# Modulation summed into columns on TensorE, and a logarithm's series moved to GpSimd, in a Griffin-style layer

## The chip, the cores and the metric

The kernel runs on one core of a Trainium2 chip, as one program. The metric is the device time of that core in microseconds, the median over several executions. Engines are called by their names in the profile: PE is TensorE (PEld its loads of the stationary operand), DVE is VectorE, ACT is ScalarE, POOL is GpSimd, SP is SyncE, which here only issues DMAs.

## The reference

One layer of a residual trunk on 1024 tokens of width 1024, all in fp32. What the change touches stands at its beginning and in the recurrent branch:

```python
c_act = jax.nn.silu(c)
mod = c_act @ w_ada[l] + b_ada[l]
shift1, scale1, gate1, shift2, scale2, gate2 = jnp.split(mod, N_MOD, axis=-1)
h = _modulated_norm(x, norm_mix_g[l], shift1, scale1)   # rmsnorm(x)*g*(1+scale) + shift
z = h @ w_in[l]
...
log_a = LRU_C * r * jax.nn.log_sigmoid(lam.astype(jnp.float32))
```

`c` is one vector of 1024, so `mod` is a vector times a 1024 x 6144 matrix. `h` feeds a product with 6144 columns, and more products, a scan, a gated mixing and a channel layer follow. `lam` is one number for each of 1024 channels.

## The kernel before, in words

Every engine has its own hand-written instruction stream; semaphores order them. Activations lie transposed, channels in partitions, 1024 tokens in the free dimension, in 8 tiles of 128 channels. Products of weights use three passes with each operand split into a high part (rounded by ScalarE, `hi(n)`, `norm_high(k)`) and a low part (the rest, by VectorE, `lo(n)`, `norm_low(k)`).

The beginning runs like this. SyncE issues `x`, rows of small parameters, then 1 MB halves of `w_ada` with weights between them. TensorE transposes `x` into `x0T`; ScalarE squares it for the norm. VectorE makes `diag0` from the roots of the mean squares, and TensorE broadcasts it (L851) so that ScalarE can keep `rbc0`, the norm's factor of each token, in all partitions.

Of the modulation four parts of 512 columns are needed at the start: part 0 and 2 are halves of the scale, 1 and 3 halves of the shift. Each is a sum over 8 pieces of 128 inputs. `PE_ROWS` gives the pieces of parts 0 and 1 that TensorE takes, as a row: `cact` is the stationary operand and 512 columns of `w_ada` move (`modulation_rows`, L827; an fp32 product is two passes in the trace). VectorE multiplies and adds the other pieces into `part_acc` (`mod_pieces`, L1975 and L1977). `add_row` (L832) adds that accumulator's column sums to the row, ScalarE copies the row to `mod_row` (`row_copy`, L1380), and `row_to_columns` (L837) turns it into four columns of 128 channels with four products. Parts 2 and 3 are all VectorE's, and `part_columns` (L814) sums their accumulators into columns. `mod_columns` (L1986) adds the bias; `scale_columns` also makes `s1`; `normed(k)` (L2007) makes the scaled norm of a tile; `norm_high` (L1384) and `norm_low` (L2012) add the shift and split.

From the first half of scale and shift on, TensorE computes the first gates (`first_gates`, L992 and L985): first those products that need channels of the first half only, then those of the second half. `keep_busy` (L822) is a product whose result nobody reads: one stands ahead of the modulation, and one between the first shift and the first gates.

For the recurrence the logarithm of a sigmoid is worked out on [128, 8] values by a series (`log_start`, `log_terms`, `log_end`, L1950 to L1968), its steps spread over VectorE's stream, each waiting for the one before. POOL makes `ident` and `ones` at the start and then sums of weights (`weight_sums`, L727 to L738), the first of them at 58 us.

Of the kernel before, what the change touches and what calls it, by code (L numbers as in the profile page):

```python
# [11 lines left out]
P = 128  # L12
# [5 lines left out]
def build(nc, a, out):  # L18
# [54 lines left out]
    with ExitStack() as ctx:  # L73
        def sem(name):
            return ctx.enter_context(nc.semaphore(name))
# [53 lines left out]
        mod_row = place("mod_row", [HALF], F32, "T", 2 * TILE + 4 * HALF)  # L129
# [115 lines left out]
        def blocks(t):  # L245
# [10 lines left out]
        rbc_kept, acc_ready, row_sum, row_ready, cols_ready, s1_ready, shift_ready = (  # L256
            sem(x) for x in ("rbc_kept", "acc_ready", "row_sum", "row_ready", "cols_ready", "s1_ready", "shift_ready"))
# [453 lines left out]
        def _(pool):  # L711
# [5 lines left out]

            def weight_sums(item, parts=(0, 1)):
# [51 lines left out]
        def _(pe):  # L770
# [46 lines left out]
            ROW_IN = (ps[3], ps[2])  # L817
            COLS = ps[3][:, 1, :]

            def keep_busy(n, tile):  # L820
                for _ in range(n):
                    nc.tensor.matmul(COLS, ident[:, :], tile, start=True, stop=True)  # L822
# [25 lines left out]
            modulation_rows(0, PE_ROWS[0])  # L848
# [469 lines left out]
        def _(act):  # L1318
# [57 lines left out]
            def row_copy(p):  # L1376
                act.wait_ge(row_sum, p + 1)
                if p:
                    act.wait_ge(cols_ready, p)
                nc.scalar.activation(mod_row[0:1, :], (ps[3], ps[2])[p][0:1, 0, :], ACT.Copy).then_inc(row_ready, 1)  # L1380

# [517 lines left out]
        def _(dve):  # L1899
# [36 lines left out]
            TERMS = 9  # L1936
# [11 lines left out]
            def log_start():  # L1948
                dve.wait_ge(lam_e, 2)
                step(V.tensor_scalar(lt[:, 2, :], lt[:, 1, :], 2.0, None, ALU.add))  # L1950
                step(V.reciprocal(lt[:, 2, :], lt[:, 2, :]))
                step(V.tensor_tensor(lt[:, 1, :], lt[:, 1, :], lt[:, 2, :], ALU.mult))
                step(V.tensor_tensor(lt[:, 2, :], lt[:, 1, :], lt[:, 1, :], ALU.mult))
# [898 lines left out]
```

## Time and profile before

| | us |
|---|---|
| median of 3 runs | 1518.69 (1518.04 to 1519.09) |
| span of the profiled execution | 1517.1 |
| TensorE busy in it | 1498.5 (99%) |
| VectorE busy | 1250.8 (82%) |
| ScalarE busy | 821.4 (54%) |
| POOL busy | 414.0 (27%) |
| first product of the first gates starts | 33.74 |

The profile shows one execution. A row of the timeline gives the start, the time from the first to the last of a run of like instructions, the engine, the line, and in brackets how long the engine had been idle and what ended that. The chain goes back from the last instruction to what released each step. A window's row gives its length, the busy time of PE, PEld, DVE, ACT and POOL with counts of instructions, and the clock that TensorE was granted as a share of 2.4 GHz.

### The profile page before, as it was taken

What the parts mean: (1) busy time and instruction counts of PE and PEld (TensorE: products, weight loads), DVE (VectorE), ACT (ScalarE), POOL (GpSimd) and SP (SyncE); (2) the same over time, 40 slices, a digit from 0 to 9 for tenths busy, and PEclk for the clock granted to TensorE, in tenths of its full rate; (3) what the DMA queues carried; (4) which work ended last, traced back from release to release, by engine and by line L of the source; (5) the groups of instructions that cost most, each with busy time, mean ns of one, the idle gap of its engine ahead of it and who ended that gap; (6) DMA issues with size and microseconds to landing.
All of it is one profiled execution on the core that took longest, in us unless ns stands there. A gap on an engine that the chain in (4) does not pass through costs nothing.

```text
span 1517.1 us, 19716 instructions
## 1 busy us (share of the span) xinstructions
PE 1498.5 (99%) x6770; PEld 1234.8 (81%) x6770; DVE 1250.8 (82%) x1577; ACT 821.4 (54%) x1222; POOL 414.0 (27%) x307
## 2 busy tenths in 40 slices
PE   7999999999999999999999999999999999999998
PEld 4888888888888888888888788888888888888887
DVE  7997888777777786698859999999999987777775
ACT  5378888734454463423446456555555553444447
POOL 0123434523213323000100433333333321333324
PEclk9999999999999999999999999999999999999999
DMA  9532233374443364573421254444444436777722
GB/s 348 186 109 62 67 91 94 116 258 129 160 149 114 102 215 146 174 231 94 167 70 35 63 165 155 153 153 153 153 153 153 153 111 232 250 250 250 250 67 112
DMA packets 212227, 231.12 MB, mean 152 GB/s; under 512 B 9920, under 2 KB 164896, under 8 KB 211360
## 3 DMA queue, kind: packets, MB, share of 16 engines
q1 hardware_dynamic: 212128, 229.86, 45.8%
q8 instruction: 55, 0.90, 0.2%
q14 instruction: 44, 0.36, 0.1%
HBM read 167.95 MB, written 61.87 MB: 151 GB/s over the span
## 4 chain that ended last, share of the span: by engine, by line
PE 92%; DVE 6%; ACT 1%; issue 1%; DMA 0%; DVEq 0%; ACTq 0%
PE ps L886 74%; PE ps L964 4%; PE ps L985 3%; PE ps L1263 1%; PE ps L1110 1%; PE ps L1245 1%; PE ps L1027 1%; PE ps L1167 1%; PE ps L1071 1%; DVE wop L1914 1%; DVE hidw L2616 1%; DVE hq L2559 1%; PE ps L814 1%; DVE n L2551 0%; PE ps L1064 0%
## 5 line engine op out<-in xcount | busy, mean ns | idle before, releaser
L1326 ACT ACTIVATE wop<-raw 128x512 fp32r<-128x512 f32 (+1 forms) x541 | 307.2, 571 | 363.6 <-PE ps L886 240.2
L1914 DVE TENSOR_TENSOR wop<-raw,wop 128x512 fp32r<-128x512 f32 (+1 forms) x541 | 376.4, 699 | 120.1 <-ACT wop L1326 118.5
L727 POOL TENSOR_TENSOR raw<-raw,raw 128x512 f32<-128x512 f32 (+1 forms) x69 | 102.4, 1484 | 868.5 <-DVE wop L1914 423.2
L886 PE MATMUL ps<-hq,wop 128*128 128x512 f32 x888 | 213.9, 390 | 1.1 <-DVE wop L1914 0.9
L886 PEld LDWEIGHTS ps<-hq,wop 128*128 128x128 f32 x888 | 166.3, 188 | 37.6 <-DVE wop L1914 1.3
L886 PE MATMUL ps<-dq,wop 128*128 128x512 f32 x840 | 190.6, 389 | 0.0
L886 PE MATMUL ps<-yq,wop 128*128 128x512 f32 x792 | 190.3, 389 | 0.0
L886 PEld LDWEIGHTS ps<-dq,wop 128*128 128x128 f32 x840 | 157.7, 188 | 32.7
L886 PEld LDWEIGHTS ps<-yq,wop 128*128 128x128 f32 x792 | 148.6, 188 | 30.9
L1928 DVE TENSOR_TENSOR ps<-ps,snap_p 128x512 f32<-128x512 f32 x136 | 94.5, 695 | 48.9 <-PE ps L886 48.3
L1341 ACT ACTIVATE snap_p<-ps 128x512 f32<-128x512 f32 x136 | 81.2, 597 | 98.9 <-PE ps L886 98.8
L2616 DVE SCALAR_TENSOR_TENSOR hidw<-ps,pc,hidw 128x1023 f32<-128x1023 f32 x96 | 122.5, 1276 | 0.9
L734 POOL TENSOR_TENSOR raw<-raw,raw 128x512 f32<-128x512 f32 (+1 forms) x69 | 91.2, 1321 | 93.7 <-DVE wop L1914 92.9
L738 POOL TENSOR_TENSOR raw<-raw,raw 128x512 f32<-128x512 f32 (+1 forms) x69 | 83.5, 1210 | 94.7 <-DVE wop L1914 93.7
L730 POOL TENSOR_TENSOR raw<-raw,raw 128x512 f32<-128x512 f32 (+1 forms) x69 | 94.1, 1363 | 9.9
L964 PE MATMUL ps<-yb_split,wop 128*128 128x512 f32 x288 | 65.7, 389 | 0.0
L1744 ACT ACTIVATE hidw<-ps,pc 128x1024 f32<-128x1024 f32 x48 | 57.5, 1207 | 15.2 <-PE ps L886 12.5
L886 PE MATMUL ps<-t2q,wop 128*128 128x512 f32 x264 | 65.1, 395 | 0.0
L886 PE MATMUL ps<-v4q,wop 128*128 128x512 f32 x264 | 63.6, 390 | 1.0 <-DVE ps L1928 1.0
L886 PE MATMUL ps<-t3q,wop 128*128 128x512 f32 x264 | 64.3, 392 | 0.0
L886 PE MATMUL ps<-t1q,wop 128*128 128x512 f32 x264 | 64.3, 392 | 0.0
L1341 ACT ACTIVATE snap_u<-ps 128x512 f32<-128x512 f32 x62 | 37.0, 598 | 50.2 <-PE ps L886 50.1
(290 smaller groups left out, 2582.2 us busy)
## 6 DMA issues: line engine op xcount, KB each, us to landing
dq<-hid_keep SPq DMA_DIRECT2D x35, 1024.0 KB, 7.3
raw<-in_w_in SPq DMA_DIRECT2D x96, 256.0 KB, 4.1
raw<-in_w_up SPq DMA_DIRECT2D x96, 256.0 KB, 3.3
hid_keep<-part_b SPq DMA_DIRECT2D x40, 512.0 KB, 3.0
hid_keep<-part_t SPq DMA_DIRECT2D x20, 512.0 KB, 3.1
raw<-in_w_down SPq DMA_DIRECT2D x80, 128.0 KB, 2.3
ada_w<-in_w_ada SPq DMA_DIRECT2D x8, 1024.0 KB, 11.4
gate_keep<-tg SPq DMA_DIRECT2D x16, 512.0 KB, 4.5
```

What stands on the lines that cost most here:

```text
L727: nc.gpsimd.tensor_tensor(s1, a21, a22, ALU.add).then_inc(s_made, 1)
L730: nc.gpsimd.tensor_tensor(a21, a11, a21, ALU.subtract).then_inc(s_made, 1)
L734: nc.gpsimd.tensor_tensor(a11, s1, a11, ALU.subtract).then_inc(s_made, 1)
L738: nc.gpsimd.tensor_tensor(s1, a12, a11, ALU.subtract).then_inc(s_made, 1)
L886: done = nc.tensor.matmul(bank, left[:, w, lk, :], right[:, x, rk, :], start=(first and w == 0 and x == 0), stop=(last and w == 1), skip_g ...
L964: done = nc.tensor.matmul(psum[:, h, :], wop[n % 4][:, w, k % KH, :], right(k, x, h), start=(k == 0 and w == 0 and x == 0), stop=(k == KT ...
L1326: nc.scalar.activation(wop[n % 4][:, 0, 0:depth[n], :], raw[slot][:, 0:depth[n], :], ACT.Copy).then_inc(f_hi, 1)
L1341: nc.scalar.activation(dst[:, :], src, ACT.Copy).then_inc(snapped, 1)
L1744: nc.scalar.activation(hidw[slot][:, 1 - s, :], flat(BANKS[pos % 2][s]), ACT.Identity, bias=C("ffn_conv_b", f), scale=C("ffn_conv_w2", f)) ...
L1914: V.tensor_tensor(wop[n % 4][:, 1, 0:kd, :], raw[slot_of[n][0]][:, 0:kd, :], wop[n % 4][:, 0, 0:kd, :].bitcast(F32), ALU.subtract).then_in ...
L1928: V.tensor_tensor(out_b, in_b, kept[:, :], ALU.add).then_inc(joined, 1)
L2616: tap = V.scalar_tensor_tensor(dst[:, d:S], src[:, 0:S - d], C("ffn_conv_w01" if k < 2 else "ffn_conv_w2", k % 2 * 2 * FT + f), dst[:, d:S ...
```

## The change

Parts 0 and 1 are no longer summed as rows. For each piece TensorE loads four 128x128 blocks of `w_ada` as stationary operands and multiplies each with one column of `cact` (`piece_columns`); the results add up in four columns of PSUM, and the accumulator's column sums are added to the same columns (`part_columns`). `mod_row`, ScalarE's two copies of it and the turning into columns are gone. Part 1 has five pieces on TensorE (2 to 6) instead of three (3 to 5), and lies in another PSUM bank than the other parts. Piece 4 of part 0 now stands behind the broadcast. VectorE takes piece 3 of part 0 ahead of the logarithm's beginning, and the order behind it is another; the series from the quotient on runs on POOL ahead of its first weight sum.

```diff
-        PE_ROWS = ((0, 1, 2, 4), (3, 4, 5), (), ())
+        PE_ROWS = ((0, 1, 2, 4), (2, 3, 4, 5, 6), (), ())
...
+        COLUMNS = [(ps[2][:, 0, :] if p == 1 else ps[3][:, 1, :])[:, KH * p:KH * p + KH] for p in range(4)]
...
+            def log_next(ins):
+                logs[0] += 1
+                ins.then_inc(log_step, 1)
+                pool.wait_ge(log_step, logs[0])
+
+            pool.wait_ge(log_root, 1)
+            log_next(nc.gpsimd.tensor_tensor(lt[:, 1, :], lt[:, 1, :], lt[:, 2, :], ALU.mult))
+            log_next(nc.gpsimd.tensor_tensor(lt[:, 2, :], lt[:, 1, :], lt[:, 1, :], ALU.mult))
+            log_next(nc.gpsimd.tensor_scalar(lt[:, 3, :], lt[:, 2, :], 1.0 / (2 * TERMS + 1), 1.0 / (2 * TERMS - 1), ALU.mult, ALU.add))
+            for j in range(TERMS - 2, -1, -1):
+                log_next(nc.gpsimd.tensor_tensor(lt[:, 3, :], lt[:, 3, :], lt[:, 2, :], ALU.mult))
+                log_next(nc.gpsimd.tensor_scalar(lt[:, 3, :], lt[:, 3, :], 1.0 / (2 * j + 1), None, ALU.add))
+            log_next(nc.gpsimd.tensor_tensor(lt[:, 3, :], lt[:, 3, :], lt[:, 1, :], ALU.mult))
+            log_next(nc.gpsimd.tensor_scalar(lt[:, 3, :], lt[:, 3, :], -2.0, None, ALU.mult))
+            log_next(nc.gpsimd.tensor_scalar(lt[:, 4, :], lam, 0.0, None, ALU.min))
+            log_next(nc.gpsimd.tensor_tensor(lt[:, 4, :], lt[:, 3, :], lt[:, 4, :], ALU.add))
+            nc.gpsimd.tensor_scalar(la4[:, :], lt[:, 4, :], LRU_C / 2, None, ALU.mult).then_inc(lru_consts, 1)
...
-            def modulation_rows(p, rows):
+            def piece_columns(p, rows):
                 for k in rows:
                     pe.wait_ge(ada_landed[p][k // KH], 16)
-                    nc.tensor.matmul(ROW_IN[p][0:1, 0, :], cact[:, k:k + 1], ada_w[p][:, k, :],
-                                     start=(k == PE_ROWS[p][0]), stop=False)
-
-            def add_row(p):
-                pe.wait_ge(acc_ready, p + 1)
-                nc.tensor.matmul(ROW_IN[p][0:1, 0, :], ones[:, 0:1], part_acc[p][:, :], start=False, stop=True).then_inc(row_sum, 1)
-
-            def row_to_columns(p):
-                pe.wait_ge(row_ready, p + 1)
-                for j in range(KH):
-                    last = nc.tensor.matmul(COLS[:, KH * p + j:KH * p + j + 1], mod_row[0:1, j * P:(j + 1) * P], ones[0:1, 0:1],
-                                            start=True, stop=True)
-                last.then_inc(cols_ready, 1)
+                    for j in range(KH):
+                        nc.tensor.matmul(COLUMNS[p][:, j:j + 1], ada_w[p][:, k, j * P:(j + 1) * P], cact[:, k:k + 1],
+                                         start=(k == PE_ROWS[p][0] and j == 0), stop=False, skip_group_check=True)
 
             def part_columns(p):
                 pe.wait_ge(acc_ready, p + 1)
-                column_sums(part_acc[p], KH, COLS[:, KH * p:KH * p + KH]).then_inc(cols_ready, 1)
+                for j in range(KH):
+                    last = nc.tensor.matmul(COLUMNS[p][:, j:j + 1], part_acc[p][:, j * P:(j + 1) * P], ones[:, 0:1],
+                                            start=not PE_ROWS[p], stop=True, skip_group_check=True)
+                last.then_inc(cols_ready, 1)
 
 
             pe.wait_ge(xT_copied[1], COPIER[:6].count(1))
             keep_busy(1, xtok[:, 0, 0:HALF])
-            modulation_rows(0, PE_ROWS[0])
+            piece_columns(0, PE_ROWS[0][:3])
             pe.wait_ge(x_diag, 1)
             for h in range(2):
                 norm = nc.tensor.matmul(ps[1][:, h, :], ones[:, :],
                                         diag0[:, HB * h:HB * h + HB, :].rearrange("p b t -> p (b t)"),
                                         start=True, stop=True)
             norm.then_inc(x_rbc, 1)
-            add_row(0)
-            modulation_rows(1, PE_ROWS[1][:1])
+            piece_columns(0, PE_ROWS[0][3:])
             pe.wait_ge(param_col, len(ROWS))
-            row_to_columns(0)
-            modulation_rows(1, PE_ROWS[1][1:])
-            add_row(1)
+            part_columns(0)
+            piece_columns(1, PE_ROWS[1])
+            part_columns(1)
             pe.wait_ge(s1_ready, 1)
-            row_to_columns(1)
...
-            row_copy(0)
-            hi(0)
-            row_copy(1)
-            hi(1)
+            for n in range(3):
+                hi(n)
             act.wait_ge(shift_ready, 1)
-            norm_high(0)
-            hi(2)
-            for k in range(1, KH):
+            for k in range(KH):
...
+                V.reciprocal(lt[:, 2, :], lt[:, 2, :]).then_inc(log_root, 1)
...
+            mod_pieces(0, (3,))
             log_start()
...
-            mod_pieces(0, (3, 5, 6, 7))
+            mod_pieces(0, (5, 6, 7))
...
-            mod_pieces(1, (0, 1, 2))
-            log_terms(7, 6)
+            mod_pieces(1, (0, 1))
             scale_columns(0)
-            mod_pieces(1, (6, 7))
             normed(0)
+            normed(1)
+            mod_pieces(1, (7,))
+            normed(2)
             lo(0)
-            normed(1)
             mod_columns(1).then_inc(shift_ready, 1)
             lo(1)
-            normed(2)
+            normed(3)
             norm_low(0)
             lo(2)
-            norm_low(1)
-            normed(3)
-            norm_low(2)
-            norm_low(3)
-            lo(3)
+            for k in range(1, KH):
+                norm_low(k)
             mod_pieces(2, range(KT))
             mod_pieces(3, range(2))
+            lo(3)
+            mod_pieces(3, range(2, KT))
+            scale_columns(2)
             lo(4)
-            scale_columns(2)
-            mod_pieces(3, range(2, KT))
             normed(4)
             mod_columns(3).then_inc(shift_ready, 1)
...
```

TensorE's stream from the first piece of the scale to the first gates, before (`ada_w_79` is part 0, `ada_w_80` part 1, `part_acc_90` and `part_acc_91` VectorE's accumulators for them; the sizes are those of the results):

```order
L827 MATMUL ps<-ada_w_79,cact 1x512 x4
L851 MATMUL ps<-diag_87,ones 128x512 x2
L832 MATMUL ps<-part_acc_90,ones 1x512
L827 MATMUL ps<-ada_w_80,cact 1x512
L837 MATMUL ps<-ones,mod_row 128x1 x4
L827 MATMUL ps<-ada_w_80,cact 1x512 x2
L832 MATMUL ps<-part_acc_91,ones 1x512
L837 MATMUL ps<-ones,mod_row 128x1 x4
L822 MATMUL ps<-ada_w_79,ident 128x512
```

And now (the accumulators are called `part_acc_89` and `part_acc_90`; the multiplier of the moving side stands first in the names):

```order
L850 MATMUL ps<-cact,ada_w_79 128x1 x12
L866 MATMUL ps<-diag_87,ones 128x512 x2
L850 MATMUL ps<-cact,ada_w_79 128x1 x4
L856 MATMUL ps<-ones,part_acc_89 128x1 x4
L850 MATMUL ps<-cact,ada_w_80 128x1 x20
L856 MATMUL ps<-ones,part_acc_90 128x1 x4
L844 MATMUL ps<-ada_w_79,ident 128x512
```

The row's three steps have become products of one column, piece 4 of part 0 has moved behind the broadcast, and part 1's pieces stand in one piece behind the scale's last columns.

VectorE's stream from part 1's first two pieces and the logarithm to the second low weight part, before:

```order
L1958 TENSOR_TENSOR lt<-lt 128x8
L1959 TENSOR_SCALAR lt<-lt 128x8
L1958 TENSOR_TENSOR lt<-lt 128x8
L1959 TENSOR_SCALAR lt<-lt 128x8
L1986 TENSOR_TENSOR mod<-ps,pc 128x4
L1931 SCALAR_TENSOR_TENSOR s_214<-mod,pc 128x4
L1977 SCALAR_TENSOR_TENSOR part_acc_91<-ada_w_80,cact,part_acc_91 128x512 x2
L2007 SCALAR_TENSOR_TENSOR tn<-x0T,s_214,rbc_89 128x1024
L1914 TENSOR_TENSOR wop_70<-raw_64,wop_70 128x512
L2007 SCALAR_TENSOR_TENSOR tn<-x0T,s_214,rbc_89 128x1024
L1986 TENSOR_TENSOR mod<-ps,pc 128x4
```

And now, from the scale's last three pieces on:

```order
L1962 SCALAR_TENSOR_TENSOR part_acc_89<-ada_w_79,cact,part_acc_89 128x512 x3
L1960 TENSOR_SCALAR part_acc_90<-ada_w_80,cact 128x512
L1962 SCALAR_TENSOR_TENSOR part_acc_90<-ada_w_80,cact,part_acc_90 128x512
L1971 TENSOR_TENSOR mod<-ps,pc 128x4
L1934 SCALAR_TENSOR_TENSOR s_213<-mod,pc 128x4
L1993 SCALAR_TENSOR_TENSOR tn<-x0T,s_213,rbc_88 128x1024 x2
L1962 SCALAR_TENSOR_TENSOR part_acc_90<-ada_w_80,cact,part_acc_90 128x512
L1993 SCALAR_TENSOR_TENSOR tn<-x0T,s_213,rbc_88 128x1024
L1917 TENSOR_TENSOR wop_70<-raw_64,wop_70 128x512
L1971 TENSOR_TENSOR mod<-ps,pc 128x4
```

The four steps on `lt` and two pieces are gone; two normed tiles now stand ahead of the last piece of part 1, and a third ahead of the first low weight part.

VectorE's stream from the last low norms of the first half to the second scale, before:

```order
L2012 SCALAR_TENSOR_TENSOR yq<-tn,mod,yq 128x2x512 x2
L1914 TENSOR_TENSOR wop_73<-raw_67,wop_73 128x512
L1975 TENSOR_SCALAR part_acc_92<-ada_w_81,cact 128x512
L1977 SCALAR_TENSOR_TENSOR part_acc_92<-ada_w_81,cact,part_acc_92 128x512 x7
L1975 TENSOR_SCALAR part_acc_93<-ada_w_82,cact 128x512
L1977 SCALAR_TENSOR_TENSOR part_acc_93<-ada_w_82,cact,part_acc_93 128x512
L1914 TENSOR_TENSOR wop_70<-raw_68,wop_70 128x512
L1986 TENSOR_TENSOR mod<-ps,pc 128x4
L1931 SCALAR_TENSOR_TENSOR s_214<-mod,pc 128x4
L1977 SCALAR_TENSOR_TENSOR part_acc_93<-ada_w_82,cact,part_acc_93 128x512 x6
```

And now:

```order
L1998 SCALAR_TENSOR_TENSOR yq<-tn,mod,yq 128x2x512 x3
L1960 TENSOR_SCALAR part_acc_91<-ada_w_81,cact 128x512
L1962 SCALAR_TENSOR_TENSOR part_acc_91<-ada_w_81,cact,part_acc_91 128x512 x7
L1960 TENSOR_SCALAR part_acc_92<-ada_w_82,cact 128x512
L1962 SCALAR_TENSOR_TENSOR part_acc_92<-ada_w_82,cact,part_acc_92 128x512
L1917 TENSOR_TENSOR wop_73<-raw_67,wop_73 128x512
L1962 SCALAR_TENSOR_TENSOR part_acc_92<-ada_w_82,cact,part_acc_92 128x512 x6
L1971 TENSOR_TENSOR mod<-ps,pc 128x4
L1934 SCALAR_TENSOR_TENSOR s_213<-mod,pc 128x4
```

The low weight part `wop_73`, which the fourth gate product reads, has moved from ahead of parts 2 and 3 to behind the second piece of part 3, and the second scale's columns from behind that piece to behind all of part 3.

## Rows read from the trace of the kernel before

**Rows 1.** The page, parts 1 (busy us, share, count) and 4 (chain).
```profile
PE 1498.5 (99%) x6770; PEld 1234.8 (81%) x6770; DVE 1250.8 (82%) x1577; ACT 821.4 (54%) x1222; POOL 414.0 (27%) x307
...
PE 92%; DVE 6%; ACT 1%; issue 1%; DMA 0%; DVEq 0%; ACTq 0%
```

**Rows 2.** The chain, 24 to 49 us: start us, us, what.
```profile
24.55 1.02 PE ps L832 x2
...
26.42 0.99 PE ps L837 x8
...
27.90 0.76 DVE part_acc L1977
...
29.36 1.28 DVE tn L2007
30.64 0.60 DVE wop L1914
31.24 1.20 DVE tn L2007
...
32.54 1.16 ACT yq L1384
...
33.74 4.60 PE ps L992 x12
38.34 10.88 PE ps L985 x48
```

**Rows 3.** The timeline, 17 to 38 us: start, us, engine, line, operation.
```profile
18.70 3.59 PE L827 MATMUL ps<-ada_w,cact 128*1 128x512 f32 x8
...
20.51 1.22 DVE L1998 TENSOR_TENSOR diag<-ident,rs 128x1024 f32<-128x1024 f32 x1
...
22.17 2.33 DVE L1977 SCALAR_TENSOR_TENSOR part_acc<-ada_w,cact,part_acc 128x512 f32<-128x512 f32 x3
22.23 1.98 PE L851 MATMUL ps<-diag,ones 128*128 128x512 f32 x4
...
24.25 1.02 ACT L1406 ACTIVATE rbc<-ps 128x1024 f32<-128x1024 f32 x1 [3.70 <-PE ps L851]
24.41 0.48 DVE L1975 TENSOR_SCALAR part_acc<-ada_w,cact 128x512 f32<-128x512 f32 x1
...
26.35 0.96 PEld L837 LDWEIGHTS ps<-ones,mod_row 1*128 1x128 f32 x8 [0.86 <-issue]
...
27.33 1.88 PE L827 MATMUL ps<-ada_w,cact 128*1 128x512 f32 x4
27.43 0.63 ACT L1326 ACTIVATE wop<-raw 128x512 fp32r<-128x512 f32 x1 [1.24 <-DMA raw<-in_w_in]
...
34.22 1.28 DVE L2012 SCALAR_TENSOR_TENSOR yq<-tn,mod,yq 128x1024 fp32r<-128x1024 f32 x1
```

**Rows 4.** Windows: busy us (count) of each engine, then PEclk, DMA share, GB/s.
```profile
13.50:16.90 3.40, 2.39 (x23) 2.15 (x21) 2.73 (x3) 3.34 (x6) 0.00 (x0) 1.00 1.05 358
...
27.16:30.57 3.41, 3.07 (x9) 0.49 (x8) 3.07 (x7) 0.65 (x2) 0.00 (x0) 1.00 1.08 363
30.57:33.98 3.41, 2.38 (x11) 1.50 (x12) 3.41 (x6) 2.53 (x4) 0.00 (x0) 1.00 1.07 372
33.98:37.39 3.41, 3.41 (x9) 2.62 (x9) 3.41 (x5) 2.31 (x3) 0.00 (x0) 0.50 1.07 376
```

**Rows 5.** Groups by line, of several stretches: busy us, mean ns, idle before.
```profile
L714 POOL TENSOR_SCALAR_AFFINE_SELECT ident<-ident 128x128 f32<-128x128 f32 x1 | 0.3, 292 | 0.2 <-POOL ident L712 0.2
...
L992 PEld LDWEIGHTS ps<-yq,wop 128*128 128x128 f32 x9 | 2.8, 313 | 0.8
...
L985 PEld LDWEIGHTS ps<-yq,wop 128*128 128x128 f32 x176 | 32.9, 188 | 7.1 <-DVE mod L1986 0.3
```

**Rows 6.** The timeline at 58 us.
```profile
57.97 2.30 POOL L727 TENSOR_TENSOR raw<-raw,raw 128x512 f32<-128x512 f32 x1 [56.29 <-DVE wop L1914]
59.03 2.32 DVE L2007 SCALAR_TENSOR_TENSOR tn<-x0T,s,rbc 128x1024 f32<-128x1024 f32 x1
```

More of the change, by code:

```diff
@@ L255, in build @@
         vch, silu_t, cact_ready, lam_e, lru_consts = (sem(x) for x in ("vector_step", "silu_t", "cact_ready", "lam_e", "lru_consts"))
-        rbc_kept, acc_ready, row_sum, row_ready, cols_ready, s1_ready, shift_ready = (
-            sem(x) for x in ("rbc_kept", "acc_ready", "row_sum", "row_ready", "cols_ready", "s1_ready", "shift_ready"))
+        rbc_kept, acc_ready, cols_ready, s1_ready, shift_ready = (
+            sem(x) for x in ("rbc_kept", "acc_ready", "cols_ready", "s1_ready", "shift_ready"))
+        log_root, log_step = sem("log_root"), sem("log_step")
         tn_ready, norm_hi, norm_lo, spilled = sem("tn_ready"), sem("norm_hi"), sem("norm_lo"), sem("spilled")
@@ L815, in column_sums @@
                 return last
-            ROW_IN = (ps[3], ps[2])
-            COLS = ps[3][:, 1, :]
             def keep_busy(n, tile):
                 for _ in range(n):
-                    nc.tensor.matmul(COLS, ident[:, :], tile, start=True, stop=True)
-            def modulation_rows(p, rows):
+                    nc.tensor.matmul(ps[3][:, 1, :], ident[:, :], tile, start=True, stop=True)
+            def piece_columns(p, rows):
                 for k in rows:
                     pe.wait_ge(ada_landed[p][k // KH], 16)
-                    nc.tensor.matmul(ROW_IN[p][0:1, 0, :], cact[:, k:k + 1], ada_w[p][:, k, :],
-                                     start=(k == PE_ROWS[p][0]), stop=False)
-            def add_row(p):
-                pe.wait_ge(acc_ready, p + 1)
-                nc.tensor.matmul(ROW_IN[p][0:1, 0, :], ones[:, 0:1], part_acc[p][:, :], start=False, stop=True).then_inc(row_sum, 1)
-            def row_to_columns(p):
-                pe.wait_ge(row_ready, p + 1)
-                for j in range(KH):
-                    last = nc.tensor.matmul(COLS[:, KH * p + j:KH * p + j + 1], mod_row[0:1, j * P:(j + 1) * P], ones[0:1, 0:1],
-                                            start=True, stop=True)
-                last.then_inc(cols_ready, 1)
+                    for j in range(KH):
+                        nc.tensor.matmul(COLUMNS[p][:, j:j + 1], ada_w[p][:, k, j * P:(j + 1) * P], cact[:, k:k + 1],
+                                         start=(k == PE_ROWS[p][0] and j == 0), stop=False, skip_group_check=True)
             def part_columns(p):
                 pe.wait_ge(acc_ready, p + 1)
-                column_sums(part_acc[p], KH, COLS[:, KH * p:KH * p + KH]).then_inc(cols_ready, 1)
+                for j in range(KH):
+                    last = nc.tensor.matmul(COLUMNS[p][:, j:j + 1], part_acc[p][:, j * P:(j + 1) * P], ones[:, 0:1],
+                                            start=not PE_ROWS[p], stop=True, skip_group_check=True)
+                last.then_inc(cols_ready, 1)
             pe.wait_ge(xT_copied[1], COPIER[:6].count(1))
             keep_busy(1, xtok[:, 0, 0:HALF])
-            modulation_rows(0, PE_ROWS[0])
+            piece_columns(0, PE_ROWS[0][:3])
             pe.wait_ge(x_diag, 1)
@@ L1374, in _ @@
                 param_copy(t)
[L1376 to L1380, printed above, removed]
             def norm_high(k):
@@ L1935, in _ @@
             lam = C("lru_lambda", 0, KT)
-            TERMS = 9
             V.memset(eps_t[:, :], EPS).then_inc(eps_made, 1)
@@ L1985, in mod_columns @@
                 c0 = (KT if p in SCALE_PARTS else 0) + p // 2 * KH
-                return V.tensor_tensor(mod[:, c0:c0 + KH], ps[3][:, 1, KH * p:KH * p + KH], C("b_ada", c0, KH), ALU.add)
+                return V.tensor_tensor(mod[:, c0:c0 + KH], COLUMNS[p], C("b_ada", c0, KH), ALU.add)
             def scale_columns(p):
@@ L2066, in _ @@
             lo(7)
-            log_terms(5)
             norm_low(5)
@@ L2079, in _ @@
             u_sum(tn[:, KH:KT, H[0]], tn[:, KH:KT, H[0]], t2w[:, :, :])
-            log_terms(4)
             lo(8)
@@ L2299, in _ @@
                         lo(n0 + w + 3)
-                    if pos == 2 and w == 6:
-                        log_terms(3, 2, 1, 0)
-                        log_end()
                     if pos in QUARTER_AT:
```

21 lines of the change are left out of this document (4 added, 17 removed).

## The prediction

> **What bounds the kernel now.** I read the page first. TensorE is busy for 99% of the span, and 92% of the chain that ended last is TensorE's [rows 1]: behind the beginning, time is saved only if TensorE starts earlier or runs faster. So I read the chain of waits from 24 us on [rows 2]. The reader is to see there how the modulation reaches the first gates: a row of sums on TensorE (24.55), turned into columns (26.42, after ScalarE's copy of the row), VectorE's last pieces of the first shift (27.90), two normed tiles (29.36, 31.24) with a weight split between them (30.64), the shift's columns behind them, ScalarE's first norm (32.54), and at 33.74 the first gates' products; from there on nearly all is TensorE. The timeline of 17 to 38 us [rows 3] has what stands beside that chain, and the windows [rows 4] have TensorE's clock: 1.00 up to 33.98, then 0.50, the lower of its two levels, up to 37.39. Before it fell TensorE did eight loads of one row with one-column products, two wide products and the first gate product.
>
> The profiled execution has a span of 1517.1 us; the median of the timed runs is 1518.69, 1.6 us more. Every difference below is worked out inside the profiled execution and added to 1518.69.
>
> **The change part by part.** *The column passes.* Four scale pieces and three shift pieces were rows of two passes of 512 columns; the first four took 3.59 us with a stop for a DMA [rows 3], 0.43 us a pass. Now each piece is four one-column products, 8 passes with a 128x128 load each. The nearest row is the turning of a row into columns: 8 loads in 0.96 us, the last of them 0.19, so 0.11 us from one to the next [rows 3], 0.89 us a piece, as much as before. Gone are both rows' passes over VectorE's accumulator (1.02 us each), ScalarE's two row copies and the turning into columns; column sums of the accumulator (8 passes) come instead.
>
> *Start of the broadcast.* The scale's pieces 0, 1, 2 end at 18.70 + 24 x 0.112 = 21.4. diag is ready at 20.51 + 1.22 = 21.73, and the broadcast no longer stands behind piece 4: it starts at 21.8, not 22.23, and ends at 23.8; ScalarE's copy (1.02 us) ends at 24.85 [rows 3].
>
> *Scale.* Piece 4 follows up to 24.5. VectorE's three remaining pieces, 2.33 us from 21.65 (piece 3 now fills its wait ahead of diag), end at 23.97 [rows 3], so they don't hold up the column sums: the last is there at 25.5, and VectorE has the scale at 25.95, where it was done with it by 27.90 before [rows 2]: 1.9 us earlier.
>
> *Shift.* TensorE has five pieces and the accumulator: 48 passes x 0.112 = 5.4 us behind 25.4, result at 30.9. The data is there: before, pieces 4 and 5 were read at 27.33 with no wait for a DMA [rows 3], and piece 4 is now due at 27.2. VectorE meanwhile does three normed tiles (1.2 us apart), one piece (0.77) and a weight split (0.68; ScalarE has its raw weights at 27.43 [rows 3]): 25.95 + 3.6 + 0.77 + 0.68 = 31.0. The two meet, so the shift is ready at 31.15 instead of 32.5, ScalarE's norm takes its 1.16 us [rows 2], and the gates start at 32.35 instead of 33.74: **1.4 us earlier**, if the clock stays at 1.00 until then. Splits 0 and 1 and the fourth tile hide beside columns, norm and filler product; ScalarE's high parts 0 to 2 fill its wait for the shift.
>
> *Later on VectorE.* Split 3 now stands behind ten pieces of the second half, and the second scale's columns behind six more. VectorE's four low norms end at 31.15 + 1.2 (two splits) + 1.2 (a tile) + 4 x 1.25 = 38.55 [rows 3]; ten pieces of 0.48 and 0.77 us end at 45.7, split 3 at 46.4, six pieces at 51.0, the columns at 51.4. With the gates at 32.35 and no slow clock TensorE needs split 3 at 49.5 and that scale at 52.2 (60, 12 and 12 passes of 0.227 us, [rows 2], and 0.9 of column sums). I price it at nothing, with 0.8 us of cover; beyond that TensorE would wait by as much as VectorE is late.
>
> *The logarithm.* Its steps on VectorE either filled waits ahead of the scale or stood beside TensorE's work: worth nothing. On POOL 27 steps follow each other, most waiting for the one before. At the price of POOL's select, 0.29 us and 0.2 of wait [rows 5], they end by 19.8 + 27 x 0.5 = 33.3; POOL's first weight sum starts at 57.97 [rows 6], which hides the rest. What they may cost is VectorE's time: beside POOL's sum of 2.30 us a normed tile took 2.32 us [rows 6], against 1.28 alone [rows 2], so 1.0 us went to 2.3 of POOL. By that share 27 steps of 0.29 us take 3.5 us, some 1.6 of it behind the scale, where VectorE is on the path; by their size (8 columns against 512) they take 27 x 0.02 = 0.5. I take 0.2 on the path, nearer the second, since the steps move hardly any data.
>
> *The clock.* This is the largest unknown. From 23.8 to 31 TensorE now does nothing but loads and one-column products. Before, passes of 512 columns stood there, and 27.16 to 30.57 has 1.00; the stretch with least of them, 30.57 to 33.98, is the one behind which the clock fell [rows 4]. No row has a stretch of full loads and one-column products alone, so I bound it. Best: they keep the clock, the new start leaves no pause, and the fall at the gates is gone too. That fall's price: the first twelve gate passes took 4.60 us [rows 2], where 12 x 0.227 is 2.7 and some 0.2 is the last one's end, so 1.7; the best is -1.4 - 1.7 = -3.1. Worst: it falls ahead of the broadcast (below). Between: it falls while the shift's columns are summed. At 0.50 a load took 313 ns, against 188 [rows 5], and a gate pass 1.9 times its time; I take 0.11 us more for a pass. With a fall near 27.2, 32 of the 48 passes are slow: +3.5. The filler product takes 1.9 us, 0.75 more than the norm that covers it: +0.75. In return the gates meet a clock that is about to rise, TensorE being dense since the filler: half of the 1.7 is saved, -0.85. With -1.4 and POOL's 0.2 the sum is -1.4 + 0.2 + 3.5 + 0.75 - 0.85 = **+2.2 us**.
>
> I take the fall during the shift's columns, since the stretch behind which the clock fell differs from those that kept it by its lack of wide passes, and the new stretch lacks them for 7 us. 1518.69 + 2.2 = **1520.9**.
>
> **The rivals.** *The columns keep the clock.* For it: the loads are nearly back to back, and the transposes of 13.50 to 16.90, loads with 128 columns each, kept 1.00 [rows 4]. Against it: 30.57 to 33.98. Time: 1518.69 - 1.2 = 1517.5 with a fall at the gates as before, 1518.69 - 3.1 = 1515.6 without. The Trainium skill, "TensorE: Matmul & The Clock Gate", Part 4, says that transposes don't count as a busy TensorE in the way that other products do; the transposes here, at 1.00, don't bear it out, and if they did, this rival would lose its best witness.
>
> *The clock falls ahead of the broadcast.* Between the filler product at 17.65 and diag at 21.73 there are only one-column passes now. If the clock is at 0.50 by 21.8, the broadcast's four passes take 0.43 us longer each, 1.7, and ten scale passes ahead of it 1.1, of which 0.4 is slack. The broadcast ends 2.4 us late; being dense it may bring the clock back, which falls again over the shift's columns: +2.2 + 2.4 = +4.6, so 1523.3. It is this case if the granted clock is 0.50 at 22 us. Against it: transposes and filler come just before.
>
> *POOL holds VectorE up.* At the upper price, 1.6 us behind the scale, the gain is gone: -1.4 + 1.6 = +0.2, so 1518.9 with the clock as before. The Trainium skill, "SBUF — State Buffer", section "Who interferes with whom", says that a VectorE instruction with two SBUF inputs contends with a GpSimd instruction that reads SBUF; every piece here is one, and the rows at 57.97 and 59.03 agree. By that rule this rival gets what chance it has.
>
> *The change doesn't shorten the chain*: if an accumulator or a landing, not TensorE, ends the shift's columns, the start stays near 33.74 and the time near 1518.7. The slack worked out above (0.5 us for the first accumulator, some 0.7 for the second, whose last piece ends at 29.2 where its sums are due at 29.9) speaks against it.
>
> **How the numbers follow.** The fall during the shift's columns 0.42 (1520.9; by when it falls, 1519 to 1523); the clock kept 0.38, half of it with the fall at the gates (1517.5) and half without (1515.6); the fall ahead of the broadcast 0.11 (1523.3); POOL or no shorter chain 0.09 (about 1518.8). The range from 1515.5 to 1523.0 leaves out most of the third case and a little of the others, under 2 in 10. A difference of 0.2%, 3.0 us, is about what a measurement of this kernel can tell from no change: faster is below 1515.65, slower above 1521.73. Faster: somewhat over half of the 0.19 without a fall, 0.11. Slower: the 0.11 and 0.16 of the 0.42, 0.27. Within: 0.62.
>
> **What would show it.** The scale read by VectorE at 25.6 shows the first half right. Then a first gate product at 32.4 means the first rival; one at 36 or later, with a granted clock of 0.50 between 24 and 31 and one-column passes some 0.21 us apart, the forecast; 0.50 at 22 us, the second rival. Pieces on VectorE of more than 0.77 us while POOL works would show the third. I am wrong if TensorE waits for split 3 or the second scale between 49 and 53 us, or if a difference arises behind 80 us.

## The result, and the profile after

The changed kernel takes 1524.76 us (median of 8 executions, 1520.64 to 1526.15), the kernel before in the same session 1518.60 (8 executions): 6.2 us more by the medians, 5.3 by the ratio of 1.0035 (95% interval 1.0026 to 1.0044). The forecast was 1520.9, the range 1515.5 to 1523.0: the time lies above the range, and the likeliest outcome, within 0.2%, did not come. Nor do the executions lie together: three took 1520.6 to 1521.5 us, five 1523.9 to 1526.2. The clock granted to TensorE, as the mean of an execution, goes with this: 0.995 in the three, 0.993 in the one of 1523.88, 0.992 in the four from 1525.6 on. The first profile is of one of the three (1521.45, 0.995), the second, taken in the experiments (e7), of a further execution, as long as the longest (1526.18, 0.992). A measured time is some 1.7 us more than its span.

The page of the changed kernel, parts 1 (busy us, share, count) and 4 (chain), for [rows 1]:

```profile
PE 1501.7 (99%) x6824; PEld 1245.9 (82%) x6824; DVE 1244.1 (82%) x1549; ACT 820.5 (54%) x1220; POOL 429.1 (28%) x334
...
PE 93%; DVE 4%; DMA 1%; SPq 1%; issue 0%; ACT 0%; DVEq 0%
```

TensorE is the bound as before, so the 6 us can only be a later start of the gates or slower passes. The timeline of TensorE and then of VectorE, first profile (start, us from first to last, engine, line, operation, idle before), for [rows 2, 3]:

```profile
18.84 2.73 PE L850 MATMUL ps<-cact,ada_w 128*128 128x1 f32 x24
21.69 1.98 PE L866 MATMUL ps<-diag,ones 128*128 128x512 f32 x4
...
25.52 2.17 PE L850 MATMUL ps<-cact,ada_w 128*128 128x1 f32 x16 [0.17 <-DMA ada_w<-in_w_ada]
28.27 5.28 PE L850 MATMUL ps<-cact,ada_w 128*128 128x1 f32 x24 [0.59 <-DMA ada_w<-in_w_ada]
33.41 1.84 PE L856 MATMUL ps<-ones,part_acc 128*128 128x1 f32 x8
35.61 2.05 PE L844 MATMUL ps<-ada_w,ident 128*128 128x512 f32 x2 [0.35 <-DVE mod L1971]
36.70 5.20 PE L1005 MATMUL ps<-yq,wop 128*128 128x512 f32 x12
...
53.44 5.75 PE L998 MATMUL ps<-yq,wop 128*128 128x512 f32 x24
...
25.50 0.49 DVE L1960 TENSOR_SCALAR part_acc<-ada_w,cact 128x512 f32<-128x512 f32 x1 [1.63 <-DMA ada_w<-in_w_ada]
...
35.30 0.16 DVE L1971 TENSOR_TENSOR mod<-ps,pc 128x4 f32<-128x4 f32 x1 [3.13 <-PE ps L856]
```

The same from the second profile, of the longer execution:

```profile
18.73 2.84 PE L850 MATMUL ps<-cact,ada_w 128*128 128x1 f32 x24
22.14 3.78 PE L866 MATMUL ps<-diag,ones 128*128 128x512 f32 x4 [0.57 <-DVE diag L1984]
...
28.99 8.67 PE L850 MATMUL ps<-cact,ada_w 128*128 128x1 f32 x40
37.52 1.84 PE L856 MATMUL ps<-ones,part_acc 128*128 128x1 f32 x8
...
40.80 5.34 PE L1005 MATMUL ps<-yq,wop 128*128 128x512 f32 x12
...
39.41 0.16 DVE L1971 TENSOR_TENSOR mod<-ps,pc 128x4 f32<-128x4 f32 x1 [4.83 <-PE ps L856]
```

The windows have the clock (length, busy us and counts of PE, PEld, DVE, ACT and POOL, then the granted clock, DMA share, GB/s): first profile, cut where the clock changes, for [rows 4],

```profile
17.87:27.09 9.22, 8.93 (x61) 7.32 (x61) 7.08 (x14) 3.61 (x9) 5.96 (x14) 1.00 1.08 366
27.09:40.74 13.65, 12.72 (x46) 10.84 (x46) 10.48 (x13) 6.68 (x8) 6.20 (x14) 0.50 1.06 364
```

and second profile:

```profile
17.77:21.23 3.46, 3.46 (x27) 2.98 (x26) 2.58 (x7) 3.04 (x9) 0.97 (x5) 1.00 1.05 387
21.23:45.12 23.89, 22.98 (x82) 18.95 (x82) 15.15 (x20) 7.70 (x9) 9.86 (x23) 0.50 1.11 375
```

Before, 3.4 us stood at 0.50; now 13.7 and 23.9 (the end of each span has 1.0 to 1.7 us more). The reader is to see that one program ran both ways: 24 column passes at the full clock take 2.73 us (0.11 each), at half 5.28 (0.22). The gates start at 36.70 and 40.80 (33.74 in [rows 2]), 2.96 and 7.06 later. The first twelve take 5.04 us (36.70 to 41.74) and 5.18 (40.80 to 45.98), against 4.44 before. What they lose, they lose in the first pass, which counts as begun while the filler product is still running at 0.50. The filler before, and the first pass by itself before, in the first and in the second profile:

```profile
32.56 1.12 PE L822 MATMUL ps<-ada_w,ident 128*128 128x512 f32 x2 [0.26 <-DVE mod L1986]
33.74 0.61 PE L992 MATMUL ps<-yq,wop 128*128 128x512 f32 x1
...
36.70 1.38 PE L1005 MATMUL ps<-yq,wop 128*128 128x512 f32 x1
...
40.80 1.39 PE L1005 MATMUL ps<-yq,wop 128*128 128x512 f32 x1
```

From the start of the first pass to that of the second it is 0.41 us before and 1.18 in both profiles, 0.77 more. The other eleven take 4.03 us before, 3.86 and 4.00 now.

From the row of 24 gate products at 53.44 to the end of the span it is 1466.3 us, in the second profile (from 57.69) 1466.8, before (from 49.87) 1467.2; in all profiles here it is 1466.2 to 1467.8. So the whole loss arises ahead of 46 us.

### The profile page after: what moved, and what is told of

Same layout as the page of the kernel before. It is cut to its first block, busy times and chain, and to the rows that moved or that the text cites. A ratio compares the mean times of both kernels' runs of the same rounds, so it can differ in the third digit from the quotient of the medians.

```text
span 1519.7 us, 19815 instructions
## 1 busy us (share of the span) xinstructions
PE 1501.7 (99%) x6824; PEld 1245.9 (82%) x6824; DVE 1244.1 (82%) x1549; ACT 820.5 (54%) x1220; POOL 429.1 (28%) x334
## 4 chain that ended last, share of the span: by engine, by line
PE 93%; DVE 4%; DMA 1%; SPq 1%; issue 0%; ACT 0%; DVEq 0%
PE ps L899 76%; PE ps L977 4%; PE ps L998 3%; PE ps L1276 1%; PE ps L1123 1%; PE ps L1258 1%; PE ps L1040 1%; DMA ada_w<-in_w_ada 1%; PE ps L1180 1%; PE ps L1084 1%; DVE wop L1917 1%; DVE hidw L2595 1%; DVE hq L2538 1%; DVE n L2530 0%; PE ps L1077 0%; PE ps L1308 0%
```

## The experiments

The theory after the result: loads with one-column products let TensorE's clock fall, and what follows at 0.50 is the loss. The rivals: POOL's steps hold VectorE up; VectorE's new order, with its landings and later splits, costs the time. Differences below are against the kernel before in the same session (medians 1518.54 to 1518.75). Clock in a table is the mean granted in an execution, lowest to highest; the kernel before has 0.998 to 1.000.

**The logarithm alone** (e1): the kernel before, with the change's steps on POOL (on semaphores that exist already, here and where rows are back):

```diff
-                step(V.reciprocal(lt[:, 2, :], lt[:, 2, :]))
-                step(V.tensor_tensor(lt[:, 1, :], lt[:, 1, :], lt[:, 2, :], ALU.mult))
...
+                V.reciprocal(lt[:, 2, :], lt[:, 2, :]).then_inc(lam_e, 1)
...
+            pool.wait_ge(lam_e, 3)
+            log_next(nc.gpsimd.tensor_tensor(lt[:, 1, :], lt[:, 1, :], lt[:, 2, :], ALU.mult))
```

> The kernel before with one part of the change alone: the logarithm's series from the quotient on runs on POOL, everything else stays. Clock theory (the loads with one-column products let TensorE's clock fall, and that is the whole loss): no one-column pieces here, so 1518.6 within 0.5 us, with the granted clock at 0.50 for about 3.4 us from 34 us on, as before. POOL theory (POOL's steps hold VectorE up ahead of the first gates): a good part of the 6.2 us, so 1520.5 to 1524.8, with VectorE's pieces at more than 0.77 us and its normed tiles at more than 1.28 us.

Measured 1518.25 (11 executions), -0.3 us, ratio 0.9997 (0.9989 to 1.0006). The timeline has POOL and VectorE side by side:

```profile
22.03 2.33 DVE L1982 SCALAR_TENSOR_TENSOR part_acc<-ada_w,cact,part_acc 128x512 f32<-128x512 f32 x3
22.14 0.73 POOL L731 TENSOR_SCALAR lt<-lt 128x8 f32<-128x8 f32 x1
...
26.48 0.23 POOL L731 TENSOR_SCALAR lt<-lt 128x8 f32<-128x8 f32 x1
...
29.23 1.28 DVE L2012 SCALAR_TENSOR_TENSOR tn<-x0T,s,rbc 128x1024 f32<-128x1024 f32 x1
```

Three pieces still take 2.33 us and a normed tile 1.28 [rows 2, 3]; it is POOL that waits (0.73 us beside the pieces for a step of 0.23). The POOL rival falls.

**The form of the sums, one at a time** (e2, e3, e5): the changed kernel with the shift, the scale or both as rows again, for instance e2

```diff
-            piece_columns(1, PE_ROWS[1])
-            part_columns(1)
+            modulation_rows(1, PE_ROWS[1])
+            add_row(1)
             pe.wait_ge(s1_ready, 1)
+            row_to_columns(1)
```

> The changed kernel with the first shift's five pieces summed as a row of 512-column passes again (row, ScalarE's copy, turning into columns), the scale as columns, VectorE's order and POOL as changed. Clock theory: passes of 512 columns stand between the broadcast and the gates, so the clock is 1.00 from 24 us until the gates; the shift is ready near 32.6 and the gates start near 33.9, hence 1518.5 to 1520; up to 1521 if the scale's columns alone let the clock fall ahead of the broadcast. Order theory (VectorE's new order with its landings and splits costs the time): 1523 to 1526 as for the changed kernel, since that order is kept.

> The changed kernel with the scale's four pieces summed as a row again and the shift's five pieces as columns. Clock theory: the clock is 1.00 up to the broadcast's end in every run and falls only while the shift's columns are summed; the runs lie together near 1521 to 1523.5 (scale about 1.5 us later than with columns, low clock some 13 us), without a group at 1525 to 1526. If the low clock ahead of the broadcast has nothing to do with the scale's columns, two groups as with the changed kernel. Order theory: 1523 to 1526.

> The changed kernel with both parts summed as rows of 512-column passes again, with its five pieces of the shift on TensorE, its order on VectorE and the logarithm on POOL kept. Clock theory: the clock is 1.00 until the gates as before; two more pieces stand in the shift's row (1.7 us, of which some 1.4 lie on the path since TensorE, not VectorE, now ends the shift), so the gates start near 35.1 and the time is 1519.3 to 1520.3, with runs within 1 us of each other. Order theory (VectorE's new order costs the time, by its landings and its later splits): 1523 to 1526.

| scale | shift | median us (executions) | lowest to highest | clock | against before |
|---|---|---|---|---|---|
| row | row (e5) | 1519.98 (11) | 1517.6 to 1520.6 | 0.998 to 0.999 | +1.4 |
| row | columns (e3) | 1520.65 (11) | 1518.6 to 1523.1 | 0.995 to 0.997 | +2.1 |
| columns | row (e2) | 1524.02 (5) | 1522.9 to 1524.3 | 0.995 | +5.5 |
| columns | columns (changed) | 1524.76 (8) | 1520.6 to 1526.2 | 0.992 to 0.995 | +6.2 |

With rows again and all else as changed (e5) the clock is 0.998 or more in every execution, against 0.995 or less in the changed kernel. In e5's profile it is 1.00 until just ahead of the gates, which start at 35.91:

```profile
17.80:35.25 17.45, 15.49 (x46) 4.71 (x46) 12.73 (x22) 7.63 (x17) 12.56 (x27) 1.00 1.08 367
35.25:38.66 3.41, 3.41 (x8) 2.20 (x7) 3.41 (x5) 3.41 (x4) 0.00 (x0) 0.50 1.05 386
```

The row is 1.4 us over before with no columns at all, as expected, though the ratio's interval (0.9996 to 1.0013) holds 1 and the executions lie wider than expected. In its profile the shift's row ends at 31.49 and its sums wait 0.18 us for VectorE's accumulator, so both engines end the shift; how the 1.4 divides between the five pieces and the order is not shown. By the medians the shift's columns cost 0.7 more, the scale's 4.1. The expectation for e2 was wrong in size: its number is the order theory's, but its rows are the clock's. In its timeline and windows

```profile
22.45 3.78 PE L885 MATMUL ps<-diag,ones 128*128 128x512 f32 x4 [0.93 <-DVE diag L2010]
```

```profile
21.80:32.04 10.24, 9.59 (x24) 5.28 (x25) 6.43 (x10) 1.65 (x2) 8.55 (x21) 0.50 1.08 356
32.04:38.87 6.83, 5.81 (x20) 1.85 (x17) 3.90 (x7) 2.49 (x4) 1.13 (x2) 1.00 1.06 376
38.87:42.28 3.41, 3.41 (x8) 2.48 (x8) 3.41 (x4) 3.41 (x5) 0.00 (x0) 0.50 1.15 320
```

the clock falls ahead of the broadcast, whose four passes take 3.78 us for 1.98; it is back only at 32.04, while the shift's wide passes run, and falls once more at the gates. e3, with the scale as a row, has 1.00 up to 30.62 in its profile:

```profile
23.60:30.62 7.02, 7.02 (x50) 5.40 (x49) 4.49 (x8) 3.50 (x5) 5.84 (x14) 1.00 1.11 350
30.62:37.44 6.82, 6.47 (x20) 4.93 (x20) 6.50 (x9) 4.01 (x4) 6.31 (x8) 0.50 1.06 373
```

Its executions spread from 1518.6 to 1523.1, further down than expected, and again with the clock: 0.997 in those up to 1519.7, 0.995 in the four at 1523. e5 keeps the new order and takes 1520: the order theory falls, but for at most 1.4 of the 6.2 us.

**The second profile** (e7): the changed kernel, unedited.

> The changed kernel once more, for a second profile. Clock theory: if this execution is one of the longer ones (1523.5 to 1526), the granted clock fell ahead of the broadcast (before 22 us) and the broadcast's passes took over 0.8 us each; if it is one of the shorter ones (1520.5 to 1521.5), it fell behind the broadcast, as in the first profile. If the longer executions owe their time to a landing instead, TensorE or VectorE waits for a DMA some 4 us longer there, and the clock is as in the first profile.

1526.18 us; its rows stand above. The clock fell at 21.23, ahead of the broadcast (22.14); a broadcast pass took 0.95 us; neither TensorE nor VectorE waited for a DMA between 19 and 42 us, though the shorter execution had such waits (1.63 us on VectorE at 25.50). A landing is not what made this long execution.

**How the parts add up** (e6, e9, e12, e11). e6 is the kernel before with its four and three pieces as columns; e9 the same with

```diff
-        PE_ROWS = ((0, 1, 2, 4), (3, 4, 5), (), ())
+        PE_ROWS = ((0, 1, 2, 4), (2, 3, 4, 5, 6), (), ())
```

e12 is the changed kernel with piece 4 of the scale ahead of the broadcast

```diff
-            piece_columns(0, PE_ROWS[0][:3])
+            piece_columns(0, PE_ROWS[0])
...
-            piece_columns(0, PE_ROWS[0][3:])
```

and e11 the changed kernel with three pieces of the shift on TensorE.

> The kernel before with one part of the change alone: its pieces (four of the scale, three of the shift) are summed as columns; VectorE's order and the logarithm are those of before. Clock theory: most of the loss is back, 1521 to 1525, with the granted clock at 0.50 for over 8 us between 18 and 40 us and runs several us apart. If columns are harmless by themselves: 1517 to 1518.8, since ScalarE's two copies and the turning into columns are gone from the chain.

> The kernel before with pieces as columns (VectorE's order and the logarithm of before, as in the run with the columns alone), and now five instead of three of the first shift's pieces on TensorE. If what the low clock costs goes with the number of loads that stand in it: 16 more passes, 0.11 us dearer each at 0.50 and no longer covered by VectorE's pieces, so 1.5 to 4 us over the run with three pieces (1520.1), 1521.6 to 1524, most runs in a group above 1523. If the changed kernel's loss has to do with VectorE's new order instead: 1519.5 to 1520.5.

> The changed kernel with one edit: piece 4 of the scale stands ahead of the broadcast again, as before. It asks where the rest lies between the changed kernel (1524.8) and the columns with five pieces in the old order (1522.4). If TensorE alone ends the shift once its clock is low, the piece now fills the wait for diag (0.57 us in the longer profile) and part of it runs at 1.00 instead of 0.50: 0.8 to 1.5 us less, 1523.3 to 1524.0. If the rest lies in VectorE's order, or in nothing but where the fall happens to lie, no difference or a longer time, 1524.5 to 1526.

> The changed kernel with three (3 to 5) instead of five of the first shift's pieces on TensorE, the other five on VectorE; all else as changed. If the low clock is paid by the loads that stand in it, 16 passes of 0.22 us leave TensorE's path (3.5 us) and VectorE gets two pieces (1.5 us, half of it in its waits): 1521.5 to 1523, and some runs below 1520. If the number of pieces doesn't matter, 1524 to 1526 as the changed kernel.

| kernel | median us (executions) | lowest to highest | clock | against before |
|---|---|---|---|---|
| columns, three pieces (e6) | 1520.11 (11) | 1518.5 to 1522.9 | 0.993 to 0.996 | +1.5 |
| columns, five pieces (e9) | 1522.39 (8) | 1521.1 to 1523.4 | 0.993 to 0.995 | +3.8 |
| and VectorE's order and POOL's logarithm (e12) | 1522.11 (10) | 1520.4 to 1524.5 | 0.992 to 0.995 | +3.4 |
| and piece 4 behind the broadcast (changed) | 1524.76 (8) | 1520.6 to 1526.2 | 0.992 to 0.995 | +6.2 |
| changed, three pieces (e11) | 1520.80 (11) | 1517.8 to 1522.9 | 0.993 to 0.996 | +2.2 |

e6 came out below its expectation, e9 within it (though three executions of eight, not most, are above 1523), e12 and e11 gained more than expected (2.8 and 4.0 us instead of 0.8 to 1.5 and 1.8 to 3.3). By the medians the columns by themselves cost 1.5 us (the ratio's interval, 1.0000 to 1.0018, begins at 1), the two more pieces 2.3, the order and POOL together nothing that can be told (-0.4), piece 4's place 2.8.

The last is not clear of the spread: the intervals of e12 (1.0014 to 1.0033) and of the changed kernel (1.0026 to 1.0044) overlap, and at the same clock the two take the same time (at 0.995 1520.4 to 1521.3 and 1520.6 to 1521.5, at 0.993 1523.7 to 1523.8 and 1523.9). They differ in how many of their executions had the clock low for long. The pieces count at the same clock too: at 0.994 e11 takes 1519.9 to 1520.8, e12 1521.9 and 1522.3. Why is in the second profile: TensorE has no pause from 22.14 until it has summed the shift, and VectorE waits 4.83 us for it. With three pieces e6's 24 passes take 5.26 us at 0.50 in its profile instead of 8.67 for 40:

```profile
26.40 5.26 PE L825 MATMUL ps<-cact,ada_w 128*128 128x1 f32 x24
```

For piece 4 one pair of profiles is all there is. In e12's the clock fell as early, at 20.93, but was back for a time behind the broadcast, as in e9's and not in the second profile of the changed kernel:

```profile
20.93:27.76 6.83, 6.83 (x22) 4.76 (x22) 4.38 (x6) 0.34 (x1) 5.72 (x14) 0.50 1.09 355
27.76:31.17 3.41, 3.41 (x32) 3.41 (x32) 2.59 (x4) 2.29 (x4) 2.90 (x7) 1.00 1.07 371
31.17:41.41 10.24, 9.89 (x34) 8.07 (x34) 8.05 (x11) 4.79 (x5) 3.04 (x5) 0.50 1.08 363
```

Whether that return is what the piece's place buys, or chance, stays open.

**Wide products among the columns** (e4): the changed kernel, with behind each of the nine pieces

```diff
+                nc.tensor.matmul(ps[3][:, 0, 0:2 * P], ident[:, :], tile, start=True, stop=True)
```

> The changed kernel with one more product of 256 columns (two passes, about 0.43 us at the full clock) behind each of the nine pieces that TensorE sums as columns; its result is read by nobody. Clock theory: the wide products keep the clock at 1.00, at 3.9 us of added passes, of which some 3.6 lie on the path: gates near 36.0 at the full clock, hence 1519 to 1521, less than the changed kernel though TensorE does more. If the clock has nothing to do with it, the added passes come on top: 1526 to 1530.

1526.17 (5 executions, clock 0.993 to 0.995), +7.6 us: a miss, and a time that the expectation gave to the case without the clock. But in its windows the clock fell all the same:

```profile
22.77:26.18 3.41, 3.41 (x6) 1.39 (x5) 2.03 (x4) 0.00 (x0) 2.81 (x8) 0.50 1.07 361
26.18:29.60 3.42, 3.42 (x29) 3.26 (x28) 0.89 (x3) 2.50 (x4) 2.49 (x12) 1.00 1.13 336
29.60:46.66 17.06, 16.71 (x58) 14.24 (x57) 9.06 (x11) 4.90 (x6) 4.64 (x6) 0.50 0.99 344
```

The expectation that 256 columns behind eight loads keep the clock falls. The time alone can't tell the added passes from the low clock; the rows have both, with 20.5 us at 0.50, from 29.60 on under the shift's columns and the gates.

**The other direction: keep the clock** (e8, e10). e8 is e1 with products that nobody reads in TensorE's pauses ahead of the gates, where before its clock fell:

```diff
+            wide(1)
             add_row(1)
             pe.wait_ge(s1_ready, 1)
+            wide(3)
             row_to_columns(1)
+            wide(1)
```

(`wide(n)` has n x 128 columns.) e10 adds the change's first step on VectorE:

```diff
             dve.wait_ge(cact_ready, 1)
+            mod_pieces(0, (3,))
             log_start()
...
-            mod_pieces(0, (3, 5, 6, 7))
+            mod_pieces(0, (5, 6, 7))
```

> The kernel before with the logarithm on POOL, and with products that nobody reads in TensorE's three pauses between 29 and 32.5 us (128, 384 and 128 columns). Clock theory: if these keep the clock at 1.00 at the first gates, the 3.4 us at 0.50 behind 34 us are gone, which cost about 1.7: 1516.5 to 1517.3, faster than either kernel. If the clock still falls at the gates, 1518.3 to 1519, the fillers costing up to 0.4.

> The kernel before with the logarithm on POOL and fillers ahead of the gates (the run that kept the clock at 1.00), and the scale's piece 3 on VectorE ahead of the logarithm's beginning, as the changed kernel has it. The piece fills VectorE's wait ahead of diag, so the accumulators of the scale and of the second half are up to 0.48 us earlier: TensorE's wait for the first (0.77 us) and for the second (0.37) shrink, 1517.4 to 1517.8 against 1518.0. If diag is held up by the piece, or a landing ends those waits, 1518.0 or more.

e8 took 1518.02 (11 executions; 0.9993, 0.9984 to 1.0002), e10 1517.69 (11; 0.9993, 0.9985 to 1.0002). Both intervals hold 1, but all executions of e10 (1516.94 to 1518.13) lie below all 24 of the kernel before in its session (1518.15 to 1519.99): its median is the shortest of all kernels here, 0.9 us below the kernel before. The clock of both is 0.999 to 1.000, and yet e8 missed what it expected for a kept clock, 1516.5 to 1517.3. The kernel before has four executions at 1.000 too; they took 1518.6 to 1520.0, no less than its others, though 3.4 us at 0.50 would leave at most 0.999. So a clock kept at the gates is not by itself a shorter time, and why these four took as long no run shows. In e10's windows and timeline

```profile
33.37:36.80 3.43, 3.43 (x15) 2.80 (x16) 3.43 (x4) 2.56 (x3) 3.18 (x4) 1.00 1.07 369
```

```profile
33.37 3.04 PE L1021 MATMUL ps<-yq,wop 128*128 128x512 f32 x12
36.25 11.04 PE L1014 MATMUL ps<-yq,wop 128*128 128x512 f32 x48
...
54.19 1.02 PE L837 MATMUL ps<-ones,part_acc 128*128 128x1 f32 x8 [0.37 <-DVE part_acc L1988]
```

the clock is 1.00 at e10's gates and the first twelve take 2.88 us (33.37 to 36.25), 1.6 less than before. e8's profile has the same (2.86), but that execution had diag 0.8 us later than e1's and started the gates at 34.51. And part is given back: at 54.19 TensorE waits 0.37 us for VectorE's accumulator of the second half, a wait that before does not have. e10's number was as expected; of the two waits it was to shorten, the first is gone and the second stayed.

## Why the prediction was wrong, step by step

The forecast failed at the clock. It had the clock fall behind the broadcast and 32 column passes run slow (+3.5). In the second profile the fall came ahead of the broadcast and no return followed until 45.12, behind the first gates: the broadcast, all 64 column passes behind it and the filler ran at 0.50. By their times and clocks most executions are like this one.

| step | forecast | first profile | second profile |
|---|---|---|---|
| column pass at 1.00 / at 0.50 | 0.11 / 0.22 us | 0.11 / 0.22 | 0.11 / 0.22 |
| broadcast starts, ends | 21.8, 23.8 | 21.69, 23.67 | 22.14, 25.92 |
| VectorE has the scale | 25.95 | 27.2 | 29.6 |
| clock falls | 27.2 | 27.09 | 21.23 |
| VectorE has the shift (31.15 + 0.2 + 3.5) | 34.85 | 35.46 | 39.57 |
| gates start (-1.4 + 0.2 + 3.5 + 0.75) | 36.8 | 36.70 | 40.80 |
| filler product | +0.75 | +0.77 | +0.77 |
| the other eleven gate passes against before | -0.85 | -0.2 | 0.0 |

**Right.** What the passes cost, the filler's 0.75, and in the shorter executions the fall during the shift's columns. The gates' start is right to 0.1 us there by luck. The filler's term is not in it: the first gate pass counts as begun 1.24 us behind VectorE's shift, as before, and waits for the filler afterwards. In that term's place stand TensorE's waits for landings (0.17 and 0.59 us), which the forecast didn't have, and POOL's 0.2 wasn't paid. VectorE has the scale late in the first profile because its pieces of part 1, which stand ahead of it, waited 1.63 us for a landing; in the second because the broadcast ran at 0.50.

**Wrong: which case is likeliest.** "The clock falls ahead of the broadcast" got 0.11, with transposes and filler just before as the reason against. By their times and clocks (0.992 in four of them, as in the second profile, 0.993 in the fifth) five of eight executions go that way. Of the eight profiles here with the scale as columns ahead of the broadcast, the clock fell ahead of it in five (e2, e4, e7, e9, e12, at 20.93 to 22.77 us), during it in two (e6, e11), and behind it only in the first. The reason given for the fall in the shift, no wide passes, held just as well for the 2.7 us of columns ahead of the broadcast; I used it only once.

**Wrong: that rival's price.** I priced it at +4.6, so 1523.3; the longer executions lie at +5.3 to +7.6. The broadcast's own part, 1.7, was right (3.78 for 1.98: 1.8). The step that failed is "being dense it may bring the clock back": it didn't in the second profile, so the scale's last 8 piece passes, its 8 accumulator passes and all 48 of the shift ran at 0.22 us, 32 more than forecast.

**Wrong: the return of the clock.** "The gates meet a clock that is about to rise", -0.85, was taken from nothing but density. The gates began at 0.50 and stayed there for 4.0 us (36.70 to 40.74) and 4.3 (40.80 to 45.12). On the eleven passes behind the first this saved 0.2 us and nothing against before. With -0.2 for -0.85 the forecast's own case comes to 1521.6; the executions of that case took 1520.6 to 1521.5.

**Wrong: what five pieces do.** The two engines were made to meet at 31.15 at the full clock, which I took as good balance; it left TensorE no cover, so each slow pass was paid in full. e11 and e9 put the two pieces at 4.0 and 2.3 us, as differences of medians of kernels that spread over 2 to 6 us.

**Right: the rivals that fell.** POOL did not hold VectorE up (e1). The chain was shortened where the clock held: TensorE's columns of the scale ended at 25.35 in the first profile (forecast 25.5). Later VectorE was harmless: no wait for split 3 or the second scale, since the gates came late. How close it is with gates at the full clock only the old order shows, in e8 and e10: there they meet the second half's accumulator and wait 0.37 us.

The Trainium skill, "TensorE: Matmul & The Clock Gate", Part 1, says that the clock's level follows how busy TensorE has been. By the profile's busy column the trace doesn't agree: in the second profile PE is busy for 22.98 of the 23.89 us at 0.50.

## What to carry to other kernels

Passes that are equal in time are not equal for the clock: before replacing 512-column passes by loads with one-column products, look which work then stands at 0.50 and whether another engine covers it. Apply a reason for a clock fall to every stretch that has it, the earliest first, and don't count on the next dense work to bring the clock back at once. Where two engines are balanced to meet at the full clock, a slow clock is paid in full. What gained here, if anything did, was to fill three short pauses with products (e8, e10): 0.6 and 0.9 us by the medians, with 1 inside both intervals. When a kernel's executions fall into groups, set each one's time beside its granted clock before explaining the median.

## What the runs showed of the hardware

- The same program ran with 13.7 us and with 23.9 us at 0.50, and its times differ by 4.7 us with it (1521.45 and 1526.18); where the fall lies varies from execution to execution (27.09 and 21.23 us), and what fixes it is not shown.
- TensorE can be busy without a pause at 0.50: from 22.14 to the end of the shift's columns at 39.4 in the second profile.
- Transposes alone went from the slow spacing to the fast one. In the kernel before TensorE does nothing else from 5.88 to 17.6 us; 20 of them take 4.42 us, and from 10.25 on 11 take 1.36. That profile's record of the clock begins at 10.09, with 1.00, so the rise is read from the spacing:

```profile
5.88 4.42 PE L801 MATMUL ps<-ident,xtok 128*128 128x128 f32 x20 [5.88 <-DMA xtok<-in_x]
...
10.25 1.36 PE L801 MATMUL ps<-ident,xtok 128*128 128x128 f32 x11
```

- POOL's steps on [128, 8] take 0.20 to 0.24 us alone and 0.67 to 0.73 beside VectorE's pieces (e1), three of which still take 2.33 us. The Trainium skill, "SBUF — State Buffer", section "Who interferes with whom", says that such a pair contends for a port that one of them holds for its whole instruction; the trace agrees, and with these short steps it was POOL that paid: no run shows a cost of them on VectorE. Beside POOL's sum of 512 columns a normed tile took 2.32 us for 1.28 [rows 2, 6].
